# Two quarters of the modulation product in column form: adaLN weights as the stationary operand

## The chip, the cores and the metric

The kernel runs on one core of a Trainium2 chip. TensorE (PE) does the matmuls, VectorE (DVE) and ScalarE (ACT) the elementwise work, SyncE's queue (SP) starts most of the DMA transfers. The metric is the device time of one execution in microseconds; the number reported is the median of several runs.

## The reference, cut to what matters

Two transformer blocks run one after the other on 256 tokens with a model width of 1024, with one layer each. The change touches only the very beginning of the first block: the modulation vectors and the normed, modulated tokens that feed the first projection.

```
m_l = (silu(c) @ w_ada + b_ada)            # latent tokens
m_c = silu(c_ctx) @ w_ada + b_ada          # context tokens
sh1, sc1, g1, sh2, sc2, g2 = split(m_l, 6) # csh1, csc1 from m_c
hl = rmsnorm(lat) * (1 + sc1) + sh1        # 256 latent tokens
hc = rmsnorm(ctx) * (1 + csc1) + csh1      # 256 context tokens
v  = h @ w_in[:, 3D:4D]                    # the value projection, first of w_in
```

Everything behind that (the gated linear recurrence, its convolutional FFN, and the whole second block) is the same in both kernels.

## The kernel before

The 512 tokens lie with channels on partitions, in 8 tiles of 128 channels by 512 tokens (`tok`). Activations and weights are split into a high and a low part (`h_hi`, `h_lo`, `w_hi`, `w_lo`) of the type fp32r, and a product is three matmuls: high by high, high by low, low by high. Weights come as a stream of chunks of 128 x 1024 through four buffers (`raw`): SP loads chunk n once the low part of chunk n-4 has been taken (`split_lo`), ACT makes the high part (`hi`, line 426), DVE the low part (`lo`, line 433), and PE multiplies. The order on each engine is written out by hand, and each engine takes its work strictly in that order; semaphores tie the engines together.

The modulation (shift and scale of the first norm, for the latent and the context vector) is made in four quarters q, each of which covers two of the eight channel tiles, for shift and scale. The input of a quarter is four tiles of `w_ada`. Quarters 0 and 1 use the plain fp32 weights that SP loads into `ada_raw`; quarters 2 and 3 come in the stream (chunks 1 to 4 and 6 to 9) and are split.

- `ada_plain(q)` (line 1166) makes quarter 0 or 1: the two condition vectors are the stationary operand (128 x 2), 512 weight columns are the moving one, and the result is two rows of 512 in one PSUM bank. It is 8 matmuls. In quarter 0 a matmul that sums the tokens' squares (line 1176, `tok_summed`) stands among them.
- `copy_rows(q)` on ACT (line 798) copies those rows to SBUF, and `turn_rows(q)` on PE (line 1192) turns them by four transposes, so that channels lie on partitions.
- `quarter(q)` on DVE (line 1615) adds the bias and makes the gains; `modulate(k)` on ACT (line 807) and `low_tokens(k)` on DVE (line 1644) then make `h_hi` and `h_lo` of channel tile k.
- `ada_rows(q)` (line 1179) makes quarters 2 and 3 from the split chunks.
- `values(j)` (line 1201) is the value projection of one chunk: 24 matmuls. `values(0)` uses chunk 0, `values(1)` chunk 5, `values(2)` chunk 10, and from then on one chunk follows the other. Work can be put between its matmuls.
- `warm(n)` (line 1157) is n matmuls of zeros, 128 x 128 x 128 in fp32. 24 of them (`WARM`) stand at the start, and 3 and 6 (`FILL`) around the turn of quarter 0.

In the trace an fp32 matmul is two records of a weight load and two of a matmul (24 matmuls of `warm` are 48 records); an fp32r matmul is one.

The order on PE is: `warm`, `ada_plain(0)`, `warm`, `turn_rows(0)`, `warm`, the first 12 matmuls of `values(0)`, `ada_plain(1)`, 9 matmuls of `values(0)`, `turn_rows(1)`, the last 3, `ada_rows(2)`, `values(1)` with `turn_rows(2)` inside, `ada_rows(3)`, `values(2)` with `turn_rows(3)` inside, and the other `values`.

Of the kernel before, what the change touches and what calls it, by code (L numbers as in the profile page):

```python
# [24 lines left out]
ACT = mybir.ActivationFunctionType  # L25
# [3 lines left out]
P = 128  # L29
D = 1024  # L30
KT = D // P
# [83 lines left out]


IDLE = 10
WARM = 24
FILL = (3, 6)
PLAIN = 2  # L120
MODS_BEHIND = (9, 12, 13, 14, 15, 16)
DIRECT = (0, 1, 5, 6)
E_QD, E_QE, E_KE, E_KD = 1, 4, 5, 6
TURN_BANKS = (6, 7, 4, 5)
HOUT_BANKS = (0, 1, 2, 4)
LOW_BANKS = (0, 1, 2, 3)
HIGH_BANKS = (4, 5, 6, 7)
# [40 lines left out]
def split_number(i):  # L168

    return i - KT + (1 if i < KT + 4 else 2)  # L170


def value_number(j):

    return 5 * j if j < 2 else KT + j
# [28 lines left out]
def build(nc, tok_in, cc_in, ada_in, stream_in, par_in, con_in, msk_in, sink_in, post_mix_in, post_mlp_in, out):  # L204
    ctx = ExitStack()
    with ctx:
        def sb(name, cols, dt=F32):
            return ctx.enter_context(nc.sbuf_tensor(name, [P, cols], dt))
# [3 lines left out]
        def S(name):  # L212
            if name not in sems:
                sems[name] = ctx.enter_context(nc.semaphore(name))
            return sems[name]
# [10 lines left out]
        xres = sb("xres", KT * T)  # L226
# [9 lines left out]
        psum = [ctx.enter_context(nc.psum_tensor(f"bank{i}", [P, 512], F32)) for i in range(8)]  # L236

        ident = con[:, 0:P]
# [6 lines left out]
        def part(cols):  # L245
            used[0] += cols
            assert used[0] <= ARENA
            return arena[:, used[0] - cols:used[0]]

        def p1(name, k=0, n=1):  # L250
            return par[:, bass.ds(k + PAR[name], n)]
# [58 lines left out]
        used[0] = TC  # L310
        mod_sum = [part(D) for _ in range(GROUPS)]
        mod_raw = [part(D) for _ in range(2 * GROUPS)]
        mod_rows = [xres[:, q * 512:(q + 1) * 512] for q in range(4)]
        ada_raw = [mod_raw[-1]] + [part(D) for _ in range(KT - 1)]
        zeros = part(P)
        used[0] = TC
# [87 lines left out]

        v_all = tok
        cs_parts = cs_w[:, :].rearrange("p (k w) -> p k w", w=4)
        def row_parts(q):
            return 2 if q < PLAIN else 4

        cs_pairs = cs.rearrange("p (k w) -> p k w", w=2)  # L410

        def move_values(engine_copy, i):
# [376 lines left out]
        def _(act):  # L789
# [7 lines left out]

            def copy_rows(q):

                if q < PLAIN:  # L800
                    act.wait_ge(S("ada_summed"), q + 1)
                else:
                    act.wait_ge(S("multiplied"), split_number(4 * q + 3) + 1)
                rows = slice(0, row_parts(q))
                act.activation(mod_rows[q][rows, :], psum[4 + q][rows, :], ACT.Copy).then_inc(S("mod_rows"), 1)

            def modulate(k):

# [23 lines left out]
            act.activation(rstd, psum[1][:, :], ACT.Ln, scale=1.0 / D, bias=eps).then_inc(S("tok_rstd"), 1)  # L832
            act.wait_ge(S("tok_rstd"), 1)
            act.activation(rstd, rstd, ACT.Exp, scale=-0.5).then_inc(S("tok_rstd"), 1)
            copy_rows(0)
            modulate(0)
            modulate(1)
            for n in range(1, 4):
                hi(act, Chunk(n))
            act.wait_ge(S("lb_diff"), 1)  # L840
            act.activation(lb_d, lb_d, ACT.Exp).then_inc(S("lb_exp"), 1)
            copy_rows(1)
            modulate(2)
            hi(act, Chunk(4))
            hi(act, Chunk(5))
# [221 lines left out]
            for t in range(TILES_IN2 + 1):  # L1067
# [20 lines left out]
                if X_FIRST < t <= X_FIRST + 8 and (t - X_FIRST) % 2 == 1:  # L1088
                    n = (t - X_FIRST) // 2
# [63 lines left out]
        def _(pe):  # L1153
# [3 lines left out]
            def warm(n):  # L1157

                for _ in range(n):
                    pe.matmul(psum[0][:, 0:P], zeros, zeros, start=True, stop=True, skip_group_check=True)  # L1160

            warm(WARM)
            pe.wait_ge(S("cs_lo"), 1)
            pe.wait_ge(S("con_in"), 16)

            def ada_plain(q):

                for i in range(4 * q, 4 * q + 4):
                    pe.wait_ge(S(f"ada_in{i}"), 16)
                    for b in range(2):  # L1170
                        k = 2 * (i % 4) + b
                        last = pe.matmul(psum[4 + q][0:2, :], cs_pairs[:, k, :], ada_raw[i][:, b * 512:b * 512 + 512],  # L1172
                                         start=k == 0, stop=k == KT - 1, skip_group_check=True)
                    if i == 1:
                        pe.wait_ge(S("tok_added"), KT - 1)
                        pe.matmul(psum[1][:, :], ones, wide[:, 0:TC], start=True, stop=True).then_inc(S("tok_summed"), 1)
                last.then_inc(S("ada_summed"), 1)
# [13 lines left out]

            def turn_rows(q):

                pe.wait_ge(S("mod_rows"), q + 1)
                n = row_parts(q)
                for m in range(4):
                    last = pe.transpose(psum[TURN_BANKS[q]][:, n * m:n * m + n], mod_rows[q][0:n, m * P:m * P + P],
                                        ident[0:n, 0:n])
                last.then_inc(S("mod_turned"), 1)

            def values(j, between={}):

                c, half = Chunk(value_number(j)), j // 4
                pe.wait_ge(S("split_lo"), c.n + 1)
                for b in range(2):
                    k = 2 * (j % 4) + b
                    for tile in range(4):
                        x = slice(k * TC + tile * P, k * TC + (tile + 1) * P)
                        dst = psum[4 * half + tile][:, :]
                        hi_w, lo_w = (w[c.slot][:, b * 512:b * 512 + 512] for w in (w_hi, w_lo))  # L1210
                        pe.wait_ge(S("h_hi"), 2 * k + 1 + tile // 2)
                        pe.matmul(dst, h_hi[:, x], hi_w, start=k == 0, stop=False, skip_group_check=True)  # L1212
                        pe.matmul(dst, h_hi[:, x], lo_w, start=False, stop=False, skip_group_check=True)  # L1213
                        pe.wait_ge(S("h_lo"), 2 * k + 2)
                        last = pe.matmul(dst, h_lo[:, x], hi_w, start=False, stop=k == KT - 1, skip_group_check=True)  # L1215
                        if k == KT - 1 and tile < 3:
                            last.then_inc(S("v_bank"), 1)
                        if (b, tile) in between:
                            between[b, tile]()
                last.then_inc(S("multiplied"), 1)  # L1220

            ada_plain(0)
            warm(FILL[0])
            turn_rows(0)
            warm(FILL[1])
            values(0, {(0, 3): lambda: ada_plain(1), (1, 2): lambda: turn_rows(1)})
            ada_rows(2)
            values(1, {(0, 2): lambda: turn_rows(2)})
            ada_rows(3)
            values(2, {(0, 2): lambda: turn_rows(3)})  # L1230
            for j in range(3, KT):
                values(j)

# [175 lines left out]
            with pe.Fori(0, (JF - FFN_PEEL) // 4) as i:  # L1409
                for u in range(4):  # L1410
                    j = FFN_PEEL + u
# [136 lines left out]
            for n in range(4):  # L1548
                pe.wait_ge(S("x_new"), n + 1)
                for j in range(4):  # L1550
                    k = 4 * (n % 2) + j
                    at = (k % 2) * T + (n // 2) * P
                    last = pe.transpose(psum[k // 2][:, at:at + P], x_tok[:, n * 512 + j * P:n * 512 + j * P + P], ident)
# [21 lines left out]
            with pe.Fori(0, (JM - MLP_PEEL) // 4) as i:  # L1575
                for u in range(4):
                    j = MLP_PEEL + u
# [8 lines left out]
        def _(dve):  # L1586
# [25 lines left out]
            def by_part(x, q):  # L1612
                return x.rearrange("p (s k) -> p s k", s=2)[:, :, 2 * q:2 * q + 2]

            def quarter(q):

                tiles, split = slice(2 * q, 2 * q + 2), q >= PLAIN
                before = 2 * q + (2 * (q - PLAIN) if split else 0)
                dve.wait_ge(S("mod_turned"), q + 1)
                n = row_parts(q)  # L1620
                turned = psum[TURN_BANKS[q]][:, 0:4 * n].rearrange("p (s k w) -> p s k w", s=2, w=n)
                b_ada = by_part(p1("b_ada", 0, ADA_FIRST), q)
                for w, dst in ((0, mod[:, 0:ADA_FIRST]), (1, mod_c)):
                    dve.tensor_tensor(by_part(dst, q), turned[:, :, :, w], b_ada, ALU.add).then_inc(S("quarter_part"), 1)
                if split:
                    for w, dst in ((0, mod[:, 0:ADA_FIRST]), (1, mod_c)):
                        dve.wait_ge(S("quarter_part"), before + w + 1)
                        x = by_part(dst, q)
                        dve.tensor_tensor(x, turned[:, :, :, w + 2], x, ALU.add).then_inc(S("quarter_part"), 1)
                done = before + (4 if split else 2)  # L1630
                for w, gain, scale in ((0, gain_l, mod), (1, gain_c, mod_c)):
                    dve.wait_ge(S("quarter_part"), done - 1 + w)
                    last = dve.scalar_tensor_tensor(gain[:, tiles], scale[:, KT + 2 * q:KT + 2 * q + 2], 1.0, p1("norm1", 2 * q, 2),
                                                    ALU.add, ALU.mult)
                last.then_inc(S("mod_first"), 1)
# [453 lines left out]
            for n in range(N_SOUT, N_MOUT):  # L2089
# [7 lines left out]
                if n == N_ROUT:  # L2097
                    dve.wait_ge(S("gate"), KT)
                    for b in range(4):
                        wait_bank(dve, 2, N_ROUT, b)  # L2100
                        x = gate_s[:, b * 512:b * 512 + 512]
                        last = dve.tensor_tensor(x, psum[HIGH_BANKS[b]][:, :], x, ALU.mult)
# [161 lines left out]
```

## Time and profile before

| | us |
|---|---|
| median of 3 runs | 920.16 |
| lowest and highest | 919.98, 921.51 |
| the profiled execution's own time | 919.98 |
| its span in the trace | 918.0 |
| PE busy | 902.8 (98%) |
| DVE busy | 653.5 (71%) |
| ACT busy | 495.3 (54%) |

The span is the time from the first to the last recorded instruction; the execution's own time is 1.98 us longer. A row of the timeline gives start, duration, engine, line, operation, what is written from what, and the count where like records are merged; in brackets stands how long the engine had been idle and what ended that.

### The profile page before, as it was taken

The numbers are of one execution on the slowest core, as the hardware profiler recorded it, in microseconds if no ns is written. First come the engines' busy times: TensorE is split into PE (matmuls) and PEld (weight loads), VectorE is DVE, ScalarE is ACT, GpSimd is POOL, SyncE is SP. The second block draws the span as 40 slices with busy tenths as digits, with TensorE's granted clock in tenths as the row PEclk, the third lists the DMA queues.
The fourth block names the chain that finished last, engine by engine and source line by source line (L and its number), as shares of the span: only waits on it lengthen the run. The fifth ranks groups of instructions, "written<-read, shape, count | busy, mean of one in ns | idle before, by whom it ended". The sixth has DMA issues, their size and how long they took to land.

```text
span 918.0 us, 17065 instructions
## 1 busy us (share of the span) xinstructions
PE 902.8 (98%) x6312; PEld 822.3 (90%) x6312; DVE 653.5 (71%) x1091; ACT 495.3 (54%) x772; POOL 0.2 (0%) x4
## 2 busy tenths in 40 slices
PE   8999999999999999999999999999999999999997
PEld 4468888888899999999999998999999889999996
DVE  4776688888887777667667988876576766555555
ACT  5543466666664755555556545445464564444443
POOL 0000000000000000000000000000000000000000
PEclk9999999999999999999999999999999999999999
DMA  9758644433425265655654543344446355555551
GB/s 346 291 211 317 227 160 138 138 137 137 137 92 184 75 212 174 203 172 175 197 176 163 185 150 122 132 161 171 161 151 214 131 185 204 185 187 191 187 186 48
DMA packets 45438, 160.93 MB, mean 175 GB/s; under 512 B 5200, under 2 KB 6608, under 8 KB 45264
## 3 DMA queue, kind: packets, MB, share of 16 engines
q1 hardware_dynamic: 43632, 156.56, 49.4%
q10 hardware_dynamic: 1760, 3.74, 1.1%
q8 instruction: 31, 0.51, 0.2%
q14 instruction: 15, 0.12, 0.0%
HBM read 159.23 MB, written 1.05 MB: 175 GB/s over the span
## 4 chain that ended last, share of the span: by engine, by line
PE 91%; ACT 3%; DVE 2%; DMA 2%; issue 1%; SPq 0%; DVEq 0%; ACTq 0%
PE bank L439 21%; PE bank L440 21%; PE bank L441 21%; PE bank L505 4%; PE bank L507 4%; PE bank L506 4%; PE bank L1212 1%; PE bank L1215 1%; PE bank L1213 1%; PE bank L1172 1%; ACT w_hi L426 1%; DMA arena<-in_ada 1%; PE bank L1265 1%; PE bank L1307 1%; PE bank L1287 1%
## 5 line engine op out<-in xcount | busy, mean ns | idle before, releaser
L433 DVE TENSOR_TENSOR w_lo<-raw,w_hi 128x1024 fp32r<-128x1024 f32 x252 | 304.3, 1222 | 136.9 <-ACT w_hi L426 136.5
L439 PE MATMUL bank<-h_hi,w_hi 128*128 128x256 f32 (+1 forms) x1232 | 368.3, 299 | 2.1 <-DVE w_lo L433 1.1
L441 PE MATMUL bank<-h_hi,w_lo 128*128 128x256 f32 (+1 forms) x1232 | 362.1, 294 | 0.0
L440 PE MATMUL bank<-h_lo,w_hi 128*128 128x256 f32 (+1 forms) x1232 | 361.6, 294 | 0.0
L426 ACT ACTIVATE w_hi<-raw 128x1024 fp32r<-128x1024 f32 x252 | 261.3, 1051 | 123.8 <-PE bank L441 87.5
L439 PEld LDWEIGHTS bank<-h_hi,w_hi 128*128 128x128 f32 x1232 | 232.4, 189 | 12.3 <-issue 2.9
L440 PEld LDWEIGHTS bank<-h_lo,w_hi 128*128 128x128 f32 x1232 | 232.4, 189 | 6.3
L441 PEld LDWEIGHTS bank<-h_hi,w_lo 128*128 128x128 f32 x1232 | 231.0, 187 | 5.9
L439 PE MATMUL bank<-y_hi,w_hi 128*128 128x256 f32 x304 | 86.4, 284 | 0.0
L441 PE MATMUL bank<-y_hi,w_lo 128*128 128x256 f32 x304 | 85.9, 283 | 0.0
L440 PE MATMUL bank<-y_lo,w_hi 128*128 128x256 f32 x304 | 85.7, 282 | 0.0
L439 PEld LDWEIGHTS bank<-y_hi,w_hi 128*128 128x128 f32 x304 | 57.5, 189 | 0.1
L440 PEld LDWEIGHTS bank<-y_lo,w_hi 128*128 128x128 f32 x304 | 57.3, 188 | 0.1
L441 PEld LDWEIGHTS bank<-y_hi,w_lo 128*128 128x128 f32 x304 | 57.0, 187 | 0.0
L505 PE MATMUL bank<-w_hi,y_hi 128*128 128x512 f32 x128 | 50.8, 397 | 0.0
L507 PE MATMUL bank<-w_hi,y_lo 128*128 128x512 f32 x128 | 50.5, 395 | 0.0
L506 PE MATMUL bank<-w_lo,y_hi 128*128 128x512 f32 x128 | 50.4, 394 | 0.0
L1128 ACT ACTIVATE y_hi<-arena 128x256 fp32r<-128x256 f32 x32 | 13.4, 419 | 43.4 <-DVE arena L2152 43.4
L990 ACT ACTIVATE arena<-arena 128x256 f32<-128x256 f32 x22 | 9.2, 418 | 42.4 <-DVE arena L1920 42.4
L507 PEld LDWEIGHTS bank<-w_hi,y_lo 128*128 128x128 f32 x128 | 24.1, 188 | 5.8
L506 PEld LDWEIGHTS bank<-w_lo,y_hi 128*128 128x128 f32 x128 | 24.2, 189 | 4.5
L505 PEld LDWEIGHTS bank<-w_hi,y_hi 128*128 128x128 f32 x128 | 24.0, 188 | 4.4
(261 smaller groups left out, 1123.6 us busy)
## 6 DMA issues: line engine op xcount, KB each, us to landing
raw<-in_stream SPq DMA_DIRECT2D x252, 512.0 KB, 3.3
arena<-in_ada SPq DMA_DIRECT2D x32, 512.0 KB, 5.5
xres<-in_ada SPq DMA_DIRECT2D x8, 512.0 KB, 3.3
tok<-in_tok SPq DMA_DIRECT2D x4, 512.0 KB, 5.6
con<-in_con ACTq DMA_DIRECT2D x1, 1472.0 KB, 9.6
xres<-in_tok ACTq DMA_DIRECT2D x1, 1024.0 KB, 8.7
out<-arena SPq DMA_DIRECT2D x4, 256.0 KB, 2.3
arena<-in_post_mix ACTq DMA_DIRECT2D x1, 512.0 KB, 4.4
```

What stands on the lines that cost most here:

```text
L426: act.activation(w_hi[c.slot][:, :], raw[c.slot][:, :], ACT.Copy).then_inc(S("split_hi"), 1)
L433: dve.tensor_tensor(w_lo[c.slot][:, :], raw[c.slot][:, :], w_hi[c.slot][:, :].bitcast(F32), ALU.subtract).then_inc(S("split_lo"), 1)
L439: pe.matmul(dst, hi_w, a_hi, start=start, stop=False, skip_group_check=True)
L440: pe.matmul(dst, hi_w, a_lo, start=False, stop=False, skip_group_check=True)
L441: return pe.matmul(dst, lo_w, a_hi, start=False, stop=stop, skip_group_check=True)
L505: pe.matmul(psum[banks[n]][:, :], a_hi[:, x], hi_w, start=start, stop=False, skip_group_check=True)
L506: pe.matmul(psum[banks[n]][:, :], a_hi[:, x], lo_w, start=False, stop=False, skip_group_check=True)
L507: last = pe.matmul(psum[banks[n]][:, :], a_lo[:, x], hi_w, start=False, stop=end, skip_group_check=True)
L990: act.activation(f_silu[p], conv[p][0], ACT.Silu).then_inc(S("f_silu"), 1)
L1128: act.activation(y_hi[:, s * T:s * T + T], u_f[p], ACT.Copy).then_inc(S("m_hi"), 1)
L1172: last = pe.matmul(psum[4 + q][0:2, :], cs_pairs[:, k, :], ada_raw[i][:, b * 512:b * 512 + 512], start=k == 0, stop=k == KT - 1, skip_grou ...
L1212: pe.matmul(dst, h_hi[:, x], hi_w, start=k == 0, stop=False, skip_group_check=True)
```

## The change

Quarters 0 and 1 are made in another form. `ada_plain(q)` becomes `ada_columns(q)`: the weights are the stationary operand, 128 x 128 at a time, and the two condition vectors are the moving one, 2 columns wide. A quarter is 32 matmuls where it was 8, and its result lies with channels on partitions in PSUM at once. So `copy_rows(0)` and `copy_rows(1)` on ACT and `turn_rows(0)` and `turn_rows(1)` on PE go, and `quarter(0)` and `quarter(1)` on DVE read the bank that the matmuls wrote and wait for the matmuls themselves (`ada_summed`).

Three other things go with it. `WARM` goes from 24 to 40 matmuls. `FILL` goes from 3 and 6 to one run of 12. And the second block of quarter matmuls stands behind 9 matmuls of `values(0)` where it stood behind 12.

```diff
-WARM = 24
-FILL = (3, 6)
-PLAIN = 2
+WARM = 40
+FILL = 12
-TURN_BANKS = (6, 7, 4, 5)
+TURN_BANKS = {2: 4, 3: 5}
...
-            copy_rows(0)
             modulate(0)
...
-            copy_rows(1)
             modulate(2)
...
-            def ada_plain(q):
+            def ada_columns(q):
...
                     for b in range(2):
                         k = 2 * (i % 4) + b
-                        last = pe.matmul(psum[4 + q][0:2, :], cs_pairs[:, k, :], ada_raw[i][:, b * 512:b * 512 + 512],
-                                         start=k == 0, stop=k == KT - 1, skip_group_check=True)
+                        for m in range(4):
+                            last = pe.matmul(psum[4 + q][:, 2 * m:2 * m + 2], ada_raw[i][:, (4 * b + m) * P:(4 * b + m + 1) * P],
+                                             cs_pairs[:, k, :], start=k == 0 and m == 0, stop=k == KT - 1, skip_group_check=True)
...
-            ada_plain(0)
-            warm(FILL[0])
-            turn_rows(0)
-            warm(FILL[1])
-            values(0, {(0, 3): lambda: ada_plain(1), (1, 2): lambda: turn_rows(1)})
+            ada_columns(0)
+            warm(FILL)
+            values(0, lambda: ada_columns(1))
             ada_rows(2)
-            values(1, {(0, 2): lambda: turn_rows(2)})
+            values(1, lambda: turn_rows(2))
...
-                dve.wait_ge(S("mod_turned"), q + 1)
+                if split:
+                    dve.wait_ge(S("mod_turned"), q - 1)
+                    turned = psum[TURN_BANKS[q]][:, 0:16].rearrange("p (s k w) -> p s k w", s=2, w=4)
+                else:
+                    dve.wait_ge(S("ada_summed"), q + 1)
+                    turned = psum[4 + q][:, 0:8].rearrange("p (s k w) -> p s k w", s=2, w=2)
```

On PE, from the start of the program to the first matmul of `values(0)` (here `arena` is the zeros or the plain `w_ada` tiles, `small` the condition vectors, `wide` the tokens' squares, `xres` the copied rows), the order before is:

```order
L1160 MATMUL bank<-arena 128x128 x24
L1172 MATMUL bank<-arena,small 2x512 x4
L1176 MATMUL bank<-wide,con 128x512
L1172 MATMUL bank<-arena,small 2x512 x4
L1160 MATMUL bank<-arena 128x128 x3
L1197 MATMUL bank<-con,xres 128x2 x4
L1160 MATMUL bank<-arena 128x128 x6
L1212 MATMUL bank<-w_hi,h_hi 128x512
```

In the changed kernel the same place of PE, with the wait of each row, reads:

```order
2 L1150 MATMUL bank<-arena 128x128 x39
3 L1163 MATMUL bank<-small,arena 128x2 [waits ada_in0,con_in,cs_lo]
4 L1163 MATMUL bank<-small,arena 128x2 x7
5 L1163 MATMUL bank<-small,arena 128x2 [waits ada_in1]
6 L1163 MATMUL bank<-small,arena 128x2 x7
7 L1167 MATMUL bank<-wide,con 128x512 [waits tok_added]
8 L1163 MATMUL bank<-small,arena 128x2 [waits ada_in2]
9 L1163 MATMUL bank<-small,arena 128x2 x7
10 L1163 MATMUL bank<-small,arena 128x2 [waits ada_in3]
11 L1163 MATMUL bank<-small,arena 128x2 x7
12 L1150 MATMUL bank<-arena 128x128 x12
13 L1202 MATMUL bank<-w_hi,h_hi 128x512 [waits h_hi,split_lo]
```

The transposes are gone, the 8 wide matmuls are 32 narrow ones, the token sum still stands in the middle, and the zeros before and behind them are more.

On ACT, between the token statistics and the second pair of modulated tiles (`tok<-tok,small` is `modulate(2)`), the order before is:

```order
L834 ACTIVATE arena<-arena 128x512
L805 ACTIVATE xres<-bank 2x512
L814 ACTIVATE h_hi<-tok,small 128x256 x4
L426 ACTIVATE w_hi<-raw 128x1024 x3
L841 ACTIVATE small<-small 128x32
L805 ACTIVATE xres<-bank 2x512
L817 ACTIVATE tok<-tok,small 128x256 x2
```

In the changed kernel it is:

```order
L826 ACTIVATE arena<-arena 128x512
L806 ACTIVATE h_hi<-tok,small 128x256 x4
L422 ACTIVATE w_hi<-raw 128x1024 x3
L832 ACTIVATE small<-small 128x32
L809 ACTIVATE tok<-tok,small 128x256 x2
```

The two copies of rows are gone, and nothing else on ACT or DVE has moved.

## Rows read from the trace of the kernel before

**Rows 1.** The page: busy time, share of the span and instructions by engine.

```profile
PE 902.8 (98%) x6312; PEld 822.3 (90%) x6312; DVE 653.5 (71%) x1091; ACT 495.3 (54%) x772; POOL 0.2 (0%) x4
```

**Rows 2.** Timeline of PE: the start, quarter 0, the fill and `values(0)`.

```profile
1.10 7.52 PE L1160 MATMUL bank<-arena 128*128 128x128 f32 x48 [1.10 <-DVE small L1607]
10.30 1.88 PE L1172 MATMUL bank<-arena,small 128*2 128x512 f32 x4 [1.69 <-DMA arena<-in_ada]
12.78 1.88 PE L1172 MATMUL bank<-arena,small 128*2 128x512 f32 x4 [0.60 <-DMA arena<-in_ada]
15.64 3.59 PE L1172 MATMUL bank<-arena,small 128*2 128x512 f32 x8
19.17 0.94 PE L1160 MATMUL bank<-arena 128*128 128x128 f32 x6
20.37 1.60 PE L1160 MATMUL bank<-arena 128*128 128x128 f32 x12
21.76 0.47 PE L1212 MATMUL bank<-w_hi,h_hi 128*128 128x512 f32 x1
```

**Rows 3.** One line's instructions (L1160), from 1 to 5 us, then 5 to 9 us.

```profile
L1160 PE MATMUL bank<-arena x18: 378/421/579, 1.1 to 4.9; 128*128 128x128 f32 x18
...
L1160 PE MATMUL bank<-arena x32: 274/275/421, 4.7 to 8.3; 128*128 128x128 f32 x32
```

**Rows 4.** Timeline of weight loads: 8 matmuls of one column on 128x128 weights.

```profile
274.51 1.87 PEld L1237 LDWEIGHTS bank<-con,xres 128*128 128x128 f32 x16
```

**Rows 5.** Timeline of ACT, DVE and PE from 16 to 25 us.

```profile
16.30 0.67 ACT L832 ACTIVATE arena<-bank,small 128x512 f32<-128x512 f32 x1
19.28 0.59 ACT L805 ACTIVATE xres<-bank 2x512 f32<-2x512 f32 x1 [1.64 <-PE bank L1172]
20.55 0.23 DVE L1624 TENSOR_TENSOR small<-bank,par 128x4 f32<-128x4 f32 x2 [1.59 <-PE bank L1197]
22.98 0.51 PE L1215 MATMUL bank<-w_hi,h_lo 128*128 128x512 f32 x1 [0.52 <-DVE h_lo L1658]
23.33 0.39 PE L1212 MATMUL bank<-w_hi,h_hi 128*128 128x512 f32 x1
25.19 0.39 PE L1215 MATMUL bank<-w_hi,h_lo 128*128 128x512 f32 x1
```

**Rows 6.** Timeline of PE, ACT and DVE around quarter 1.

```profile
25.51 7.03 PE L1172 MATMUL bank<-arena,small 128*2 128x512 f32 x16
32.47 0.51 PE L1212 MATMUL bank<-w_hi,h_hi 128*128 128x512 f32 x1
35.22 0.23 DVE L1624 TENSOR_TENSOR small<-bank,par 128x4 f32<-128x4 f32 x2 [3.45 <-PE bank L1197]
35.91 0.39 PE L1187 MATMUL bank<-w_hi,cs_w 128*4 128x512 f32 x1
```

**Rows 7.** Timeline of ACT, DVE and PE between quarter 1 and `values(2)`.

```profile
39.77 0.40 PE L1187 MATMUL bank<-w_hi,cs_w 128*4 128x512 f32 x1 [0.92 <-DVE w_lo L433]
40.91 0.51 PE L1212 MATMUL bank<-w_hi,h_hi 128*128 128x512 f32 x1
41.02 0.57 ACT L805 ACTIVATE xres<-bank 4x512 f32<-4x512 f32 x1
51.99 0.50 PE L1212 MATMUL bank<-w_hi,h_hi 128*128 128x512 f32 x1 [0.95 <-DVE w_lo L433]
```

**Rows 8.** The chain that ended last, 43 to 52 us: start, length, what.

```profile
43.82 5.77 DMA raw<-in_stream
...
50.71 1.24 DVE w_lo L433
```

**Rows 9.** A stage: us, PE PEld DVE ACT POOL busy, PEclk, DMA, GB/s.

```profile
916.00:918.00 2.00, 0.00 (x0) 0.00 (x0) 0.00 (x0) 0.00 (x0) 0.00 (x0) 0.61 0.48 177
```

**Rows 10.** Timeline of PE: the last matmul of the program.

```profile
912.07 0.39 PE L507 MATMUL bank<-w_hi,y_lo 128*128 128x512 f32 x1
```

**Rows 11.** The page, DMA issues: KB each, median us from issue to landing.

```profile
raw<-in_stream SPq DMA_DIRECT2D x252, 512.0 KB, 3.3
```

More of the change, by code:

```diff
@@ L312, in build @@
         mod_raw = [part(D) for _ in range(2 * GROUPS)]
-        mod_rows = [xres[:, q * 512:(q + 1) * 512] for q in range(4)]
+        mod_rows = {q: xres[:, q * 512:(q + 1) * 512] for q in TURN_BANKS}
         ada_raw = [mod_raw[-1]] + [part(D) for _ in range(KT - 1)]
@@ L406, in build @@
         cs_parts = cs_w[:, :].rearrange("p (k w) -> p k w", w=4)
-        def row_parts(q):
-            return 2 if q < PLAIN else 4
         cs_pairs = cs.rearrange("p (k w) -> p k w", w=2)
@@ L798, in copy_rows @@
             def copy_rows(q):
[L800 to L805, printed above, removed]
+                act.wait_ge(S("multiplied"), split_number(4 * q + 3) + 1)
+                act.activation(mod_rows[q][0:4, :], psum[4 + q][0:4, :], ACT.Copy).then_inc(S("mod_rows"), 1)
             def modulate(k):
@@ L1192, in turn_rows, with values @@
             def turn_rows(q):
-                pe.wait_ge(S("mod_rows"), q + 1)
-                n = row_parts(q)
+                pe.wait_ge(S("mod_rows"), q - 1)
                 for m in range(4):
-                    last = pe.transpose(psum[TURN_BANKS[q]][:, n * m:n * m + n], mod_rows[q][0:n, m * P:m * P + P],
-                                        ident[0:n, 0:n])
+                    last = pe.transpose(psum[TURN_BANKS[q]][:, 4 * m:4 * m + 4], mod_rows[q][0:4, m * P:m * P + P],
+                                        ident[0:4, 0:4])
                 last.then_inc(S("mod_turned"), 1)
-            def values(j, between={}):
+            def values(j, between=None):
                 c, half = Chunk(value_number(j)), j // 4
@@ L1217, in values @@
                             last.then_inc(S("v_bank"), 1)
-                        if (b, tile) in between:
-                            between[b, tile]()
+                        if b == 0 and tile == 2 and between is not None:
+                            between()
                 last.then_inc(S("multiplied"), 1)
-            ada_plain(0)
-            warm(FILL[0])
-            turn_rows(0)
-            warm(FILL[1])
-            values(0, {(0, 3): lambda: ada_plain(1), (1, 2): lambda: turn_rows(1)})
+            ada_columns(0)
+            warm(FILL)
+            values(0, lambda: ada_columns(1))
             ada_rows(2)
-            values(1, {(0, 2): lambda: turn_rows(2)})
+            values(1, lambda: turn_rows(2))
             ada_rows(3)
-            values(2, {(0, 2): lambda: turn_rows(3)})
+            values(2, lambda: turn_rows(3))
             for j in range(3, KT):
@@ L1615, in quarter @@
             def quarter(q):
-                tiles, split = slice(2 * q, 2 * q + 2), q >= PLAIN
-                before = 2 * q + (2 * (q - PLAIN) if split else 0)
-                dve.wait_ge(S("mod_turned"), q + 1)
-                n = row_parts(q)
-                turned = psum[TURN_BANKS[q]][:, 0:4 * n].rearrange("p (s k w) -> p s k w", s=2, w=n)
+                tiles, split = slice(2 * q, 2 * q + 2), q in TURN_BANKS
+                before = 2 * q + (2 * (q - 2) if split else 0)
+                if split:
[4 more added lines that the diff above has]
+                    turned = psum[4 + q][:, 0:8].rearrange("p (s k w) -> p s k w", s=2, w=2)
                 b_ada = by_part(p1("b_ada", 0, ADA_FIRST), q)
```

## The prediction

> **What bounds the kernel now.** The page first: PE is busy 98% of the span [rows 1]. So a change of a few microseconds must be followed on PE, and the question is when PE gets through the opening. From the chain of waits the place to watch is 51.99 us, where `values(2)` begins: PE had waited 0.95 us there for the low part of chunk 10 [rows 7], and that chunk's own chain is a load issued at 43.82 us, then ACT's high part, then DVE's low part from 50.71 [rows 8]. Behind 51.99 the list of waits shows PE none for the rest of the opening, because loads, ACT and DVE follow PE's own progress from there. I take the end of the program to move as the start of `values(2)` moves. Next read the timeline of PE: 24 matmuls of zeros, quarter 0 from 10.30 to 19.17 us, fill and turn, `values(0)` from 21.76 [rows 2], quarter 1 from 25.51 to 32.47 [rows 6].
>
> **The matmuls.** A wide matmul is two records: quarter 1 is 8 matmuls, 16 records, in 32.47 - 25.51 = 6.96 us, 0.435 us a record [rows 6]. The new form's nearest relative is the one-column matmul on full weights: 16 records of weight load take 1.87 us, the last one's own length of some 0.19 included, so one starts every 0.112 us [rows 4]. A new quarter is 32 matmuls, 64 records: 64 x 0.112 = 7.2 us. It is a quarter of the time for each matmul and four times the matmuls: +0.2 us a quarter. A second column adds nothing I can see, since the weight load sets the pace.
>
> **The extra zeros.** Warm zeros start at the same pace. The 48 records end at 8.62 us, and PE then stood idle for 1.69 us until the first weight tile landed at 10.30 [rows 2]. 16 more matmuls are 32 records, 3.6 us, so the first quarter starts at 12.1 instead of 10.30. Half of the addition fills an idle gap, half (1.8 us) is delay.
>
> **Quarter 0.** Before, from 10.30 to 19.17, it had another idle stretch of 0.60 for the second tile [rows 2], which is there by 12.78. After, it has none: 7.2 us and the token sum of 1.0 (14.66 to 15.64 between the rows around it) make it end at 12.1 + 8.2 = 20.3. The statistics that need the token sum come about 1.1 us later; ACT's logarithm began at 16.30 [rows 5] and so goes to about 16.9, and its followers are done before 20.3, so this costs nothing. What the missing copy and turn give: before, the copy ran at 19.28 for 0.59 and DVE's `quarter(0)` began at 20.55, 1.4 us behind PE's last weight matmul [rows 2, 5]. After, DVE begins once the last record has drained, about 20.55 again. The delay of the zeros has eaten the gain of the missing copy.
>
> **The fill.** 12 records of fill stood from 20.37 to 21.76, 0.116 each [rows 2]. Now 24 records follow 20.3: 2.9 us with the change of operands, to 23.2. `h_hi` and `h_lo` of tile 0 are there by 22.98 as before [rows 5], so the wait of 0.52 us goes, and fill is what PE is late by: `values(0)` starts at 23.2 instead of 21.76.
>
> **Quarter 1.** 9 matmuls of `values(0)` at 0.233 each (8 from 23.33 to 25.19 [rows 5]) take 2.1 us, so the block runs from 25.4 to 32.6. DVE's `quarter(1)` can start at 32.9; before it started at 35.22 [rows 6], as PE put 9 more matmuls and the transposes ahead of it. This is the real gain: 2.3 us for everything that hangs on tiles 2 and 3, the low part of chunk 4 included, for which PE waited 0.92 us at 39.77 [rows 7].
>
> **PE from there.** The other 15 matmuls of `values(0)` end at 32.6 + 3.6 = 36.2 (before 35.91 [rows 6]). `ada_rows(2)` took 40.91 - 35.91 less the wait of 0.92, 4.0 us with rounding, and now ends at 40.2. `values(1)` and `ada_rows(3)` took 51.99 - 0.95 - 40.91 = 10.1 with the tail of the last matmul, 10.0 without [rows 7]: PE is ready for `values(2)` at 50.2, **1.8 us early**. Is chunk 10 ready? Its issue waits for the low part of chunk 6, which on ACT stands behind `copy_rows(2)`, at 41.02 [rows 7]; that copy waits for the end of `ada_rows(2)`, 40.2, so it gains only 0.7 us, not 2.3. With an unchanged 5.77 us for the load, chunk 10 would allow a start at 51.3. But a load takes 3.3 us in the median [rows 11]; this one stood behind loads that are now issued 2.3 us earlier. I take 1.8 us and keep 0.7 as the lower end.
>
> **The granted clock.** All these prices hold at 2.4 GHz. The first 18 records of zeros last 421 ns, and later ones 275 [rows 3]: that is the level of 1.2 GHz until about 5.1 us, after some 4.0 us of matmuls from 1.10. At the end, after the last matmul from 912.07 to 912.46 [rows 10], the stage from 916 to 918 shows 0.61 [rows 9], a mix of the whole and the half: it fell at about 916.4. So in this run the clock fell after PE had streamed nothing for 4.0 us, and in the opening it was held through idle gaps of 1.69 and 0.60. What no row shows is a stretch as long as 7.2 us with weight loads back to back and almost nothing streamed: the one-column matmuls last 1.9 us at a time [rows 4]. A wide matmul streams 512 columns; 64 new records stream 2 each, 128 columns against 8192. If what counts is what streams, the block looks nearly idle, and I take that as likelier than not, for the one fall in the trace came with nothing streamed, and every stretch that held the clock streamed wide operands within it.
>
> Its price, from rows at either level: the 18 slow records of zeros from 1.10 to 4.9 start 0.21 us apart [rows 3], the warm weight loads 0.112 [rows 4], so a record at the half clock costs 0.10 more. The bounds are none and all of the 64 records of quarter 1, 0 and 6.4 us. I take 28 of them, 2.8 us, a little under the middle, since the block begins at the whole clock. Behind the block `values(0)` starts at half clock; at the start of the program 4.0 us of matmuls went by at half speed before it rose [rows 3], so 2.0 us. Together 4.8 us on PE. Chunk 10 (51.3 at the latest before, and pushed back by no more than PE's 4.8) then costs nothing more, as it has less in front of it: `values(2)` starts at 50.2 + 4.8 = 55.0, 3.0 later than 51.99.
>
> **The sum.** Against the profiled execution's own 919.98 us: 919.98 - 1.8 + 4.8 = 923.0. The median of the runs is 0.18 above that execution: **923.2 us**.
>
> **Rivals.**
> (a) The clock holds. In the new blocks PE is never idle, and the one fall in the trace came with PE idle [rows 9, 10]. Then the sum is 920.16 - 1.8 = 918.3 us, or 919.5 if chunk 10 keeps its load time. It decides on whether loads without streaming count as work. The Trainium skill, TensorE: Matmul & The Clock Gate, section Why this matters for your kernels, asks only that PE has no idle gaps between bursts, by which this rival's 918.3 would hold; the same page, Part 4: PE-mode transpose, says that transposes do not count as busy in the same way, which speaks for the forecast. No run here shows either yet.
> (b) The clock falls in quarter 0 as well. It has two blocks of 3.6 us around a token sum of 1.0 us. At half clock from the token sum on: 1.0 for the sum, 32 x 0.101 = 3.2 for the second block, and 18 records of fill, 1.8: 6.0 us more, and then quarter 1 as forecast. 923.2 + 6.0 = 929.2 us. For it: `WARM` now ends right at the block, so nothing has streamed from 12.1 to 15.7. Against: its stretches are half as long as quarter 1, and the token sum streams 512 columns twice.
> (c) The narrow matmuls pay more than their weight load, for instance in changes of operand. The dearest fp32 records of full weights in the rows are the 6 of the first fill, 0.94 us or 0.157 each [rows 2], 0.045 above my price: with 128 new records 5.8 us, and 924.1 us without any fall. It decides from 0.014 a record on, where the 1.8 us are gone. Against it: the 12 records of the second fill take 0.116 each.
>
> **Chances.** Clock falls in quarter 1 alone 0.38, in both 0.20, holds 0.35, (c) and others 0.07. The range reaches from 917.6 (a little under a, for the 0.52 us wait that my sum folds into the fill) to 930 (a little over b), the own range of the forecast from 920.4 (no slow record, 2.0 for the matmuls behind) to 926.8 (all 64). A measurement here tells apart about 0.2%, 1.8 us. Case (a) lies on that border: of its 0.35 I give 0.14 to faster, and 0.21 to the same. Of the forecast 0.10 lies within 0.2%; of (c) one third each. Faster 0.17, same 0.32, slower 0.51.
>
> **What would show it.** A granted clock below 1.00 in a stage between 25 and 42 us, and the changed kernel's narrow records more than 0.112 apart there, show the fall; if the stages from 12 to 20 us show it too, it is (b). 1.00 throughout, quarter 1 done at about 32.6 and `values(2)` at about 50.2 us show (a). `values(0)` not before 23.2 us shows the price of zeros and fill right. The forecast is wrong if PE reaches `values(2)` before 51.99, or if PE waits for a chunk behind it where it waited for none before.

## The result, and the profile after

The changed kernel is slower: 929.44 us in the median of 4 runs (928.84 to 930.14), against 920.84 us of the kernel before in the same comparison (919.98 to 921.63, 4 runs). The ratio is 1.0094, 95% interval 1.0077 to 1.0111. The prediction forecast slower, 923.2 us, in a range of 917.6 to 930. The measured time lies in the range, at its upper end: it is that of rival (b), 929.2 us.

First the page of the changed kernel: busy time by engine, and the granted clock (PEclk) in 40 slices of the span. It answers [rows 1].

```profile
span 927.6 us, 17315 instructions
...
PE 916.4 (99%) x6438; PEld 848.3 (91%) x6438; DVE 653.0 (70%) x1091; ACT 494.1 (53%) x770; POOL 0.2 (0%) x4
...
PEclk8699999999999999999999999999999999999999
```

The span has grown by 9.6 us (918.0 before), PE is busy for 13.6 us more, and DVE and ACT do the same as before. `values(2)` begins at 61.69 us, 9.7 later than before [rows 7], so the whole loss lies in front of it. The first two slices show where: the clock was not whole in the first 46 us. The stages of that stretch follow (length, busy time of PE, PEld, DVE, ACT, POOL, then PEclk, DMA share, GB/s). Between 20 and 28 us, left out here, PE was busy throughout at 0.50.

```profile
12.00:15.00 3.00, 3.00 (x30) 3.00 (x28) 1.38 (x2) 0.41 (x1) 0.00 (x0) 1.00 1.05 411
15.00:17.00 2.00, 2.00 (x10) 1.48 (x11) 0.71 (x1) 1.06 (x1) 0.00 (x0) 0.70 1.00 392
17.00:20.00 3.00, 3.00 (x14) 2.48 (x13) 1.35 (x3) 1.32 (x2) 0.00 (x0) 0.50 1.03 410
...
28.00:30.00 2.00, 2.00 (x11) 1.91 (x11) 2.00 (x4) 1.85 (x2) 0.00 (x0) 0.64 1.03 410
30.00:32.00 2.00, 2.00 (x13) 1.69 (x11) 2.00 (x3) 0.00 (x0) 0.00 (x0) 1.00 0.80 297
32.00:36.00 4.00, 4.00 (x38) 4.00 (x37) 3.64 (x8) 0.23 (x1) 0.00 (x0) 1.00 0.94 326
36.00:40.00 4.00, 4.00 (x22) 4.00 (x22) 0.00 (x0) 0.00 (x0) 0.00 (x0) 0.53 0.17 69
40.00:44.00 4.00, 4.00 (x13) 3.32 (x13) 2.40 (x7) 1.73 (x3) 0.00 (x0) 0.50 0.00 0
44.00:46.00 2.00, 2.00 (x6) 1.57 (x5) 0.05 (x1) 0.00 (x0) 0.00 (x0) 0.50 0.00 0
```

PE is busy in every one of them, without a pause, and yet the clock falls to its half (1.2 GHz) twice: in quarter 0, at about 15.8 us (0.70 in the stage from 15 to 17), and in quarter 1, at about 36.3. The timeline of PE in the same stretch shows what that costs. It answers [rows 2, 6].

```profile
1.09 11.31 PE L1150 MATMUL bank<-arena 128*128 128x128 f32 x80 [1.09 <-DVE small L1595]
12.24 3.63 PE L1163 MATMUL bank<-small,arena 128*128 128x2 f32 x32
15.73 2.01 PE L1167 MATMUL bank<-wide,con 128*128 128x512 f32 x2
17.54 6.83 PE L1163 MATMUL bank<-small,arena 128*128 128x2 f32 x32
24.22 5.41 PE L1150 MATMUL bank<-arena 128*128 128x128 f32 x24
29.34 0.52 PE L1202 MATMUL bank<-w_hi,h_hi 128*128 128x512 f32 x1
...
31.57 9.36 PE L1163 MATMUL bank<-small,arena 128*128 128x2 f32 x64
40.79 0.77 PE L1202 MATMUL bank<-w_hi,h_hi 128*128 128x512 f32 x1
41.36 0.63 PE L1203 MATMUL bank<-w_lo,h_hi 128*128 128x512 f32 x1
41.79 0.63 PE L1205 MATMUL bank<-w_hi,h_lo 128*128 128x512 f32 x1
```

The first 32 narrow records take 3.6 us at the whole clock; the next 32, the same work, take 6.8 at the half. The 24 records of fill take 5.4 us, where 2.8 are enough at the whole clock (`wide_same` below). Quarter 1 takes 9.2 us, and the matmuls of `values(0)` behind it start 0.43 us apart where they were 0.23.

### The profile page after: what moved, and what is told of

Its sections match the earlier page's. It is cut to its first block, busy times and chain, and to the rows that moved or that the text cites. A ratio compares the mean times of both kernels' runs of the same rounds, so it can differ in the third digit from the quotient of the medians.

```text
span 927.6 us, 17315 instructions
## 1 busy us (share of the span) xinstructions
PE 916.4 (99%) x6438; PEld 848.3 (91%) x6438; DVE 653.0 (70%) x1091; ACT 494.1 (53%) x770; POOL 0.2 (0%) x4
## 3 DMA queue, kind: packets, MB, share of 16 engines
q10 hardware_dynamic: 1760, 3.74, 1.1%
## 4 chain that ended last, share of the span: by engine, by line
PE 93%; ACT 3%; DVE 2%; issue 1%; DMA 1%; DVEq 0%; ACTq 0%
PE bank L435 21%; PE bank L436 21%; PE bank L437 20%; PE bank L501 4%; PE bank L503 4%; PE bank L502 4%; PE bank L1163 2%; PE bank L1150 2%; PE bank L1202 2%; PE bank L1205 1%; PE bank L1203 1%; ACT w_hi L422 1%; PE bank L1253 1%; PE bank L1295 1%; PE bank L1291 1%
```

## The experiments

Each kernel was timed beside the kernel before on the same chip. "Pair" is the pair of condition vectors, the moving operand of the column form.

| run | ratio to before, 95% interval | median us, before us | `values(2)` begins, us |
|---|---|---|---|
| the change | 1.0094 (1.0077 to 1.0111) | 929.44, 920.84 | 61.69 |
| wide_same | 0.9983 (0.9973 to 0.9992) | 918.89, 920.56 | 50.46 |
| wide_short | 0.9972 (0.9959 to 0.9984) | 918.34, 920.56 | 51.77 |
| narrow_q0 | 1.0079 (1.0061 to 1.0098) | 929.35, 920.56 | 60.15 |
| narrow_q1 | 1.0046 (1.0033 to 1.0059) | 925.62, 920.56 | 56.20 |
| warm40 | 1.0008 (0.9998 to 1.0019) | 922.32, 920.91 | 54.36 |
| place9 | 1.0005 (0.9995 to 1.0016) | 921.60, 920.91 | 53.91 |
| moving32 | 1.0093 (1.0077 to 1.0108) | 930.05, 920.91 | 61.28 |
| wide_mid | 0.9959 (0.9946 to 0.9973) | 917.73, 920.91 | 49.68 |
| wide0_narrow1 | 1.0033 (1.0021 to 1.0044) | 923.58, 920.45 | 55.77 |
| moving64 | 0.9983 (0.9970 to 0.9995) | 919.33, 920.45 | 50.41 |

The last column is from one profiled execution each; before has 51.99 there [rows 7]. It carries a scatter of its own: behind the same 40 zero matmuls quarter 0 began at 11.66 us in one execution (`moving64`) and at 12.93 in another (`warm40`). So the price of a fall is counted below from the start of a block.

### Is it what the blocks stream?

The theory: the clock falls because the narrow blocks stream almost nothing. The rival: it falls for another reason in the column form, and the time would be lost with any moving operand. The edit to the changed kernel leaves every weight load in its place and only repeats the pair. In short:

```diff
-psum[4 + q][:, 2 * m:2 * m + 2]     <- weights tile, cs_pairs[:, k, :]               # 2 columns
+psum[4 + q][:, 128 * m:128 * m + 128] <- weights tile, the pair 64 times, step 0     # 128 columns
```

> The changed kernel in all but one thing: the moving operand of the column form is the pair of condition vectors repeated 64 times (128 columns) instead of 2 columns, written to a PSUM slice of 128 columns; 40 and 12 zero matmuls and the place behind 9 matmuls as in the changed kernel. Theory A (the clock fell because the blocks stream almost nothing): granted clock 1.00 in every stage from 6 us on, the narrow blocks' records still 0.112 us apart since the weight load sets the pace, quarter 0 done at about 20.3 us, quarter 1 at 32.6, values(2) at 50 to 51 us, time 918.3 to 919.5 against 920.2 of before. Theory B (full-width fp32 weight loads, or the order of the work, bring the clock down whatever streams): clock 0.50 from about 16 us as in the changed kernel, time 928 to 930. Theory C (a narrow matmul costs more than its load even at the full clock): clock 1.00 but records 0.12 to 0.16 apart, 920 to 924.

Measured: 918.89 us, ratio 0.9983, beyond its interval and on the other side of before. Of its timeline of PE, quarter 0, the fill, the first of `values(0)`, quarter 1, and the start of `values(2)`:

```profile
11.73 3.74 PE L1190 MATMUL bank<-small,arena 128*128 128x128 f32 x32
15.30 1.02 PE L1198 MATMUL bank<-wide,con 128*128 128x512 f32 x2
16.16 4.03 PE L1190 MATMUL bank<-small,arena 128*128 128x128 f32 x32
20.02 2.84 PE L1165 MATMUL bank<-arena 128*128 128x128 f32 x24
22.62 0.48 PE L1236 MATMUL bank<-w_hi,h_hi 128*128 128x512 f32 x1
24.81 7.31 PE L1190 MATMUL bank<-small,arena 128*128 128x128 f32 x64
31.88 0.48 PE L1236 MATMUL bank<-w_hi,h_hi 128*128 128x512 f32 x1
...
50.46 0.50 PE L1236 MATMUL bank<-w_hi,h_hi 128*128 128x512 f32 x1 [1.11 <-DVE w_lo L436]
```

And the granted clock in the stage of quarter 1:

```profile
28.00:32.00 4.00, 4.00 (x38) 4.00 (x38) 3.91 (x9) 0.36 (x2) 0.00 (x0) 1.00 1.02 405
```

Here 64 records with 128 moving columns take 7.1 us from their start to that of the next matmul, about what 64 with 2 columns would take at the whole clock (7.2 by the rows of before). Streaming the other 126 columns costs next to nothing (3.74 us for 32 records against 3.63 in the changed kernel), with the weight loads (PEld) busy for all of the stage, and the clock stays whole. One property of the operand was changed and the whole loss went, so the rival falls. A narrow matmul that is dear in itself falls too, by the changed kernel's own first 32 records: they take 3.49 us up to the token sum (12.24 to 15.73), 0.109 each.

Two runs lie between 2 and 128 columns; the edit is only that number.

> The changed kernel with the pair repeated to 32 moving columns, between the 2 of the changed kernel and the 128 of the run that held the clock; 40 and 12 zeros. The theory that what streams decides gives no number of its own for it: either 1.00 throughout and 918.5 to 919.5 like 128 columns, or a fall and up to 930 like 2 columns. The rival that a 2-column matmul is special (its form, not how much it streams) gives 1.00. Records 0.112 apart at the whole clock, 0.21 at half, in either case.

Measured: 930.05 us, as slow as with 2 columns. So it is not a special case of a 2-column matmul. The stage of quarter 1:

```profile
32.00:36.00 4.00, 4.00 (x29) 4.00 (x29) 3.65 (x8) 0.23 (x1) 0.00 (x0) 0.73 0.90 293
```

> The changed kernel with the pair repeated to 64 moving columns, 40 and 12 zeros: between 32 columns (fell, 930) and 128 (held, 918.9). No number of its own follows; held gives 918.5 to 919.5, fallen in both quarters 929 to 930, anything between says that it depends on the execution.

Measured: 919.33 us, as fast as with 128 columns. The clock is whole in quarter 1 of the profiled execution (918.15 us):

```profile
28.00:32.00 4.00, 4.00 (x39) 4.00 (x37) 3.91 (x9) 0.46 (x2) 0.00 (x0) 1.00 1.02 406
```

The two slowest of the ten runs, 920.82 and 921.70 us, had a mean granted clock of 0.997 and 0.996 where the others had 0.998 to 1.000, so a short fall in some executions is not ruled out.

### What is each fall worth?

Three kernels have one narrow quarter each. The first keeps the changed kernel's shape and streams 128 columns in quarter 0, 2 in quarter 1, which is just the case that the prediction forecast.

```diff
-MOVING = 2              # both quarters
+MOVINGS = (128, 2)      # quarter 0, quarter 1
```

> The changed kernel with quarter 0 streaming 128 columns and quarter 1 streaming 2, with 40 and 12 zeros. This is the case that the blind prediction forecast (a fall in quarter 1 alone). From the traces so far: quarter 0 as in the run with 128 columns (values(0) at about 22.6), quarter 1 and the matmuls behind it as in the changed kernel's own quarter 1 (from 31.57 to 40.9, and 12 or more slow matmuls behind): values(2) at 54 to 56, time 923 to 925. If the two falls are not additive and quarter 1 falls only after a fall in quarter 0: 918.5 to 919.5.

Measured: 923.58 us, ratio 1.0033. Timeline of PE, quarter 1 and the first slow matmul behind it, then two stages of it:

```profile
25.36 9.29 PE L1190 MATMUL bank<-small,arena 128*128 128x2 f32 x64
34.51 0.77 PE L1236 MATMUL bank<-w_hi,h_hi 128*128 128x512 f32 x1
```

```profile
28.00:30.00 2.00, 2.00 (x20) 2.00 (x20) 1.97 (x6) 0.31 (x2) 0.00 (x0) 1.00 1.03 412
30.00:32.00 2.00, 2.00 (x12) 2.00 (x12) 2.00 (x4) 0.00 (x0) 0.00 (x0) 0.53 1.02 401
```

The clock is whole until about 30.1 us and falls once, in quarter 1, although it had not been low shortly before. From the start of quarter 1 to `values(2)` it takes 55.77 - 25.36 = 30.41 us, and the kernel with 128 columns in both quarters 50.46 - 24.81 = 25.65: the fall in quarter 1 costs 4.8 us. From the start of quarter 0 to that of quarter 1 the changed kernel takes 31.57 - 12.24 = 19.33 us and the kernel with 128 columns 24.81 - 11.73 = 13.08: the fall in quarter 0 costs 6.2 us. The medians say nearly the same, 923.58 - 918.89 = 4.7 and 929.44 - 923.58 = 5.9 us.

The other two start from the kernel before and make only one quarter in column form with 2 columns; the zeros, the fill and the place behind 12 matmuls stay.

> The kernel before with quarter 1 alone in column form (2 moving columns), behind 12 matmuls, no copy and turn for it; quarter 0 in the row form with its turn, 24 zeros and fill of 3 and 6. Theory A: the clock falls once, inside quarter 1, as the blind forecast had it: 4 to 6 us of slow records and matmuls on PE less up to 1.8 us of waits that are filled: 922 to 925. Theory B the same. If quarter 1 fell in the changed kernel only because the clock had been low shortly before: clock 1.00, 919 to 920.

Measured: 925.62 us. The fall in quarter 1 is there, as in the run above, but the median is 2 us dearer. In the profiled execution (926.35 us) PE then waited 2.30 us for chunk 10 in front of `values(2)`, and the clock fell a second time, from 57.7 to 61.1 us.

```profile
56.20 0.51 PE L1236 MATMUL bank<-w_hi,h_hi 128*128 128x512 f32 x1 [2.30 <-DVE w_lo L436]
```

The nine runs fit that: three took 923.0 to 923.4 us at a mean granted clock of 0.993 or 0.994, as the run above did (923.58 us, 0.994), and six took 925.50 to 927.35 us at 0.989 to 0.992. So the second fall seems to come in some executions only.

> The kernel before with quarter 0 alone in column form (2 moving columns), 24 zeros, fill of 3 and 6 back to back behind it, quarter 1 in the wide row form behind 12 matmuls. Theory A: the clock falls in quarter 0 and rises again in the fill or values(0); the price is that of the fall in quarter 0 alone, about 6 us less 1 to 2 of missing copy and zeros: 923 to 927. If the fall in quarter 0 of the changed kernel hung on its later place behind 40 zeros: clock 1.00 there, about 919 to 920.

Measured: 929.35 us, dearer than expected by 2.3 to 6.3 us. The fall came already at 12.9 us, before the block was half done, and lasted to 30.0, and here too a second one followed from 60.7 to 64.1, behind a wait of 2.37 us. One of its four runs, 926.39 us at a clock of 0.990, was as cheap as expected; the others took 929.33 to 929.49 at 0.987. Its timeline of PE shows in what the block differs from the changed kernel's: it starts behind an idle gap and has another inside. Whether the gaps brought the earlier fall was not tried.

```profile
10.42 1.92 PE L1190 MATMUL bank<-small,arena 128*128 128x2 f32 x16 [1.34 <-DMA arena<-in_ada]
12.90 3.57 PE L1190 MATMUL bank<-small,arena 128*128 128x2 f32 x16 [0.56 <-DMA arena<-in_ada]
16.34 2.05 PE L1198 MATMUL bank<-wide,con 128*128 128x512 f32 x2
```

So the price of quarter 0 in this shape is not that of the changed kernel, and the two single prices do not add up to the change's 8.6 us. The two that share its shape do: 4.8 + 6.2 us, less the 1.5 by which `wide_same` begins `values(2)` sooner than before, is 9.5, against the 9.7 us by which the changed kernel begins it later.

### The extra zeros and the place

Each is one number in the kernel before.

```diff
-WARM = 24
+WARM = 40
```

> The kernel before with 40 instead of 24 zero matmuls at the start and nothing else changed. By the blind sum quarter 0 starts at 12.1 instead of 10.3 us and everything behind it is up to 1.8 us later, less the 0.60 us of a wait for the second weight tile that goes: values(0) at 22.9, time 921 to 922. Rival: the waits between quarter 1 and values(2) (0.92 and 0.95 us) are set by transfers and take the delay up: 920 to 920.8. In both the clock is 1.00 throughout.

Measured: ratio 1.0008 (0.9998 to 1.0019), 922.32 against 920.91 us: inside its interval, so no loss is shown by the time. The trace shows a loss within the opening: quarter 0 begins at 12.93, `values(0)` at 23.62 instead of 21.76, `values(2)` at 54.36. That is 2.4 us later than in the profile of before, while the span is 2.5 us longer. Of it 0.8 is owed to the zeros of this execution, behind which quarter 0 begins at 12.93 where the prediction has 12.1. The median of the comparison is 1.4 us above before.

```diff
-values(0, {(0, 3): lambda: ada_plain(1), (1, 2): lambda: turn_rows(1)})
+values(0, {(0, 2): lambda: ada_plain(1), (1, 2): lambda: turn_rows(1)})
```

> The kernel before with quarter 1 behind 9 instead of 12 matmuls of values(0), nothing else. By the blind sum DVE's quarter(1) comes no earlier, as its turn stays where it was behind 21 matmuls; values(2) at 51.99 as before, time the same within 0.1%. If the place alone gave the gain of the wide-moving runs: 918.5 to 919.5.

Measured: ratio 1.0005 (0.9995 to 1.0016), no difference in time, as expected. Its profiled execution (922.31 us) holds a surprise: `values(2)` begins 1.9 us later than in the profile of before, and the row form lost the clock too, behind the idle gap in front of the first weight tile. Timeline of PE, then the stages:

```profile
10.33 5.33 PE L1172 MATMUL bank<-arena,small 128*2 128x512 f32 x8 [1.97 <-DMA arena<-in_ada]
...
53.91 0.50 PE L1212 MATMUL bank<-w_hi,h_hi 128*128 128x512 f32 x1 [1.89 <-DVE w_lo L433]
```

```profile
10.00:12.00 2.00, 1.67 (x4) 0.28 (x4) 1.39 (x2) 0.50 (x2) 0.00 (x0) 0.85 1.03 420
12.00:14.00 2.00, 2.00 (x4) 0.21 (x3) 1.38 (x2) 0.56 (x1) 0.00 (x0) 0.50 1.03 418
```

With a gap of 1.97 us the clock fell at about 11.4; with one of 1.69 us in the profile of before it held [rows 2], and so it did behind the gap of 1.89 us in front of `values(2)` in this same execution. Since nothing in front of the first gap was changed, the kernel before can have this fall in some executions, which would be one reason for its spread (919.4 to 923.4 us in this comparison). No profile of before shows it. Its granted clocks leave it open: of its seven runs above 922 us two had 0.996, but five had 0.998, as some of the quick ones did.

### A faster kernel

With 128 columns the column form's own gain can be looked for, with fewer zeros.

```diff
-WARM = 40
-FILL = 12
+WARM = 24
+FILL = 6
```

> As the run with 128 moving columns, but with 24 zero matmuls at the start and 6 behind quarter 0. Theory A: clock 1.00, quarter 0 starts at 10.3 and ends at about 19.2, DVE's quarter(0) at 19.5 instead of 20.55, values(0) at about 20.9 instead of 21.76, values(2) 1 to 2 us earlier than in the run with 40 and 12: 917 to 918.5. Theory B: clock falls, over 925.

Measured: ratio 0.9972, 918.34 us, but with single runs from 917.23 to 920.91. The profiled one (920.91) had two falls, each behind an idle gap of PE, of 2.69 us in front of quarter 0 and of 2.00 in front of `values(2)`:

```profile
11.09 5.44 PE L1190 MATMUL bank<-small,arena 128*128 128x128 f32 x32 [2.69 <-DMA arena<-in_ada]
...
51.77 0.50 PE L1236 MATMUL bank<-w_hi,h_hi 128*128 128x512 f32 x1 [2.00 <-DVE w_lo L436]
```

```profile
12.00:14.00 2.00, 2.00 (x11) 2.00 (x11) 0.84 (x2) 1.06 (x1) 0.00 (x0) 0.50 1.03 420
...
52.00:54.00 2.00, 2.00 (x7) 1.51 (x7) 1.91 (x4) 0.87 (x1) 0.00 (x0) 0.61 0.00 0
```

So the last kernel covers both gaps with zeros: enough at the start to reach the first weight tile, and four where PE waits for chunk 10.

```diff
-WARM = 24
-FILL = 6
+WARM = 32
+FILL = 9
...
             ada_rows(3)
+            warm(4, 6)      # four zero matmuls into bank 6, free here
```

> A candidate for a faster kernel: 128 moving columns, 32 zero matmuls at the start (to about 10.3 us, so that no long idle gap is left before the first weight tile), 9 behind quarter 0, and 4 zeros into a free bank behind the second split quarter, where PE waits 1 to 2 us for chunk 10. Expected: clock 1.00 throughout in all executions, values(0) at about 21.5, values(2) at 49.3 to 50, time 917 to 918 with less spread than the run with 24 and 6. If the 1.1 us wait for chunk 10 grows by what PE gains (the load is the bound): 918.5 like the run with 40 and 12.

Measured: 917.73 us, ratio 0.9959 (0.9946 to 0.9973), and the five runs lie between 917.60 and 917.93. That is faster than both kernels. Which of the three edits did how much was not tried. Timeline of PE:

```profile
1.09 9.97 PE L1165 MATMUL bank<-arena 128*128 128x128 f32 x64 [1.09 <-DVE small L1632]
10.90 3.93 PE L1190 MATMUL bank<-small,arena 128*128 128x128 f32 x32
...
47.91 1.05 PE L1165 MATMUL bank<-arena 128*128 128x128 f32 x8
49.68 0.50 PE L1236 MATMUL bank<-w_hi,h_hi 128*128 128x512 f32 x1 [0.72 <-DVE w_lo L436]
```

Of the 3.2 us between the medians, 2.3 are the earlier `values(2)` (51.99 to 49.68). I leave open whether the rest is the fall behind the start gap that some executions of before may have.

## Why the prediction came out as it did

**Direction and mechanism.** The step that decided was the granted clock, and it was right: a block of weight loads that streams next to nothing loses the clock though PE is never idle. The argument was that the only fall in the trace of before came with nothing streamed [rows 9, 10] and that all stretches that held it streamed wide operands. The runs with 32, 64 and 128 columns, whose weight loads are the same, show that what streams made the difference here.

**The step that failed** is the chance of a fall in quarter 0, not a term's price. I set its two stretches of 3.6 us around a token sum against one of 7.2 us and gave "in both" 0.20, "in quarter 1 alone" 0.38. The clock fell at 15.8 us in the changed kernel, at the end of the first stretch. So the forecast of 923.2 us was 6.2 us low; that the range still held 929.44 us is owed to rival (b), and "slower" had been given no more than 0.51. In `wide0_narrow1`, which is the forecast's own case, the forecast was close: `values(2)` at 55.0 forecast and 55.77 measured, 923.2 us forecast and 923.58 measured.

**The terms**, as the prediction put them, beside the trace of the changed kernel (for the terms at the whole clock, of `wide_same`):

| term | forecast us | measured us |
|---|---|---|
| quarter 0 starts | 12.1 | 12.24 (`wide_same` 11.73) |
| 64 narrow records at the whole clock | 7.2 | 31.88 - 24.81 = 7.1 with 128 columns |
| `values(0)` starts, clock whole | 23.2 | 22.62 |
| fall in quarter 0, on the start of `values(0)` | 6.0 (rival b) | 29.34 - 22.62 = 6.7, of it 0.5 the later start of quarter 0 |
| quarter 1 with slow records | 7.2 + 2.8 = 10.0 | 40.79 - 31.57 = 9.2 |
| slow matmuls behind it | 2.0 | some 13 at 0.43 for 0.23, 2.6 |
| `values(2)`, clock whole (rival a) | 50.2 | 50.46 |
| `values(2)`, both falls (rival b) | 55.0 + 6.0 = 61.0 | 61.69 |

The forecast's 28 slow records were too many: quarter 1's excess of 2.0 us makes some 20 at 0.10 each. The slow matmuls behind were more than I took, and the two errors cancel; that the price of the fall came out at the 4.8 us of the forecast is in part luck. In rival (b) all 24 records of fill were slow where the prediction had 18.

**The missing copy and turn.** The gain of the change was real: at the whole clock, with its zeros and fill, the column form begins `values(2)` 1.5 us sooner (51.99 to 50.46; forecast 1.8, lower end 0.7) and runs at 0.9983 of before. Rival (a) at 918.3 us was thus close for a kernel that holds the clock; `wide_same` took 918.89. Its 50.2 us for `values(2)` came near 50.46 by two errors that cancel: PE was ready at 49.35, 0.9 us sooner than forecast, and then waited 1.11 for chunk 10, for which the sum had nothing.

**Chunk 10.** The prediction took the low part of chunk 4 to come 2.3 us sooner with `quarter(1)`, and PE to wait for nothing in front of `values(2)` after a fall. Both failed: in `wide_same` DVE began that low part 1.7 us sooner (36.82 against 38.49 us), and in the changed kernel PE waited 0.83 us. ACT may make a chunk's high part only once PE has let go of the buffer, for chunk 4 the end of `values(0)`; in the code that stands in `hi`, and I had not followed it. In the changed kernel the timeline of ACT and PE shows the wait:

```profile
47.23 2.01 ACT L422 ACTIVATE w_hi<-raw 128x1024 fp32r<-128x1024 f32 x2 [3.98 <-PE bank L1205]
```

ACT stood idle 3.98 us for the last matmul of `values(0)` (L1205), and behind it come the chunks that lead to chunk 10. So the slow matmuls are paid for on this chain as well, and PE still waits for chunk 10. In `wide_same` the same wait is 1.28 us and PE's for chunk 10 is 1.11, above the 0.95 of before: some of the sooner quarter 1 ends there.

**A busy PE.** In the changed kernel PE was busy for all of 12 to 46 us, and the clock stood at 0.50 in much of it. The Trainium skill, TensorE: Matmul & The Clock Gate, section Why this matters for your kernels, asks for no idle gaps of PE between bursts. Here that was not enough, and where the Trainium skill and these runs differ, the runs decide. What the Trainium skill says in Part 4: PE-mode transpose of the same title, that transposes do not count as busy in the same way, points the right way but speaks of another instruction.

**What stays open.** That the streamed columns hold the clock is shown for this opening. Whether weight loads count for nothing or for a little was not tried, nor was where between 32 and 64 columns the outcome changes. The forecast's rival (c), a dearer narrow matmul, was at 0.045 a record above 0.112; the changed kernel's first 32 narrow records, 0.109 each, show none of it. Why a gap of 1.89 us did not bring a fall and one of 1.97 us did was not tried either.

## What to carry to other kernels

A small matrix by vector product can have its weights as the stationary or as the moving operand at the same price on TensorE (here 6.96 us a quarter in the row form and 7.1 in the column form, in fp32); the column form saves the copy and the turn, but with the vector as it is the array streams 2 columns a weight load, and here the granted clock fell and what followed paid too. Repeating the vector with a step of zero, under the weight load that sets the pace anyway, cost next to no time, and with 64 or 128 columns (not with 32) the clock held. In an opening, look at the granted clock by stages before believing a busy PE. Zeros in gaps of about 2 us are worth a try: with them the runs lay between 917.60 and 917.93 us, without them between 917.23 and 920.91.

## What the runs showed of the hardware that was not expected

- The clock fell with PE busy throughout: at about 15.8 and 36.3 us in the changed kernel, with 2 columns moving per 128 x 128 fp32 weight load; likewise with 32 columns (930.05 us). With 64 and 128 it held in the profiled executions (medians 919.33 and 918.89 us).
- In fp32, 128 moving columns take hardly more time than 2 behind a full weight load: 3.74 us for 32 records, against 3.63 us for 32 with 2 columns at the whole clock.
- Idle gaps of PE of 1.97, 2.00, 2.30, 2.37 and 2.69 us in the opening were each followed by a fall, while gaps of 1.89 us (`place9`), 1.69 us [rows 2] and 1.55 us (`moving32`) were not.
- After each fall in the opening the clock stayed at the half while PE was already working on wide operands again: in the changed kernel from 40.79, when the wide matmuls began, to about 46.5 us.
